# Two-layer hybrid encoder on one core: recurrent periods of layer 0 in another order on every engine, latent keys normed by columns, the last output norm inside the attention, band and maximum fused in layer 1

## What is computed

```python
# mixer A
c_kv = rmsnorm(c_kv, kv_gain)                    # 1024 rows of 128
score = einsum(w, relu(einsum(q_idx, k_idx)));   _, idx = top_k(score, 256)
p = softmax(einsum(q @ w_uk, c_kv[idx]));        o = (p @ c_kv[idx]) @ w_uv
# mixer B, per chunk of 64 rows and head (4 heads)
a_mat = strict(beta * k @ k.T * decay)
u, w = triangular_solve(a_mat + eye, [v * beta, k * beta * exp(g)])
v_new = u - w @ state
o = (q * exp(g)) @ state + (q @ k.T * decay) @ v_new
state = state * exp(g_last) + (k * exp(g_last - g)).T @ v_new
o = rmsnorm(o, out_gain) * silu(z)
# mixer D (layer 1), per chunk: keys of two chunks, 8 heads, sink per head
s = q @ k.T / 8;  s = where(valid, s, -inf);  p = softmax([s, sink])[:-1];  o = p @ v
```

## Time and profile before

| | us |
|---|---|
| median of 3 runs | 2655.8 |
| lowest, highest | 2655.26, 2657.01 |
| profiled execution: its own time | 2654.52 |
| profiled execution: span | 2652.8 |
| mean granted clock of PE over the span | 0.973 |
| busy over the span: PE, DVE, ACT, POOL | 2513.3, 1586.7, 1013.8, 213.5 |
| recurrence, first operation of PE to the last query | 359.5 to 638.7 |
| attention of layer 0 | 645 to 848 |
| window attention of layer 1 | 1798 to 1864 |

### The profile page before, as it was taken

How to read it: one execution, slowest core, us unless ns; L and a number is a source line. 1 busy time by engine, 2 the same in 40 slices (tenths; PEclk the granted TensorE clock), 3 DMA queues, 4 the chain that set the end, 5 groups by cost and what they waited for, 6 DMA issues and landing times.

```text
span 2652.8 us, 33869 instructions
## 1 busy us (share of the span) xinstructions
PE 2513.3 (95%) x13062; PEld 1976.0 (74%) x13062; DVE 1586.7 (60%) x2585; ACT 1013.8 (38%) x1816; POOL 213.5 (8%) x242
## 2 busy tenths in 40 slices
PE   7999978888988999999999998997999999999998
PEld 5587757776555878888888786784778888888787
DVE  6389966754553576565643556638577566653444
ACT  4323323444443443333332333527443333332333
POOL 4025523220000000000010000000000000000000
PEclk8999988897999999999999999999999999999999
DMA  5121100000001332222255342110232232326342
GB/s 178 39 72 44 51 10 10 2 33 1 1 24 63 96 111 90 85 86 74 83 177 184 120 155 62 34 48 17 80 127 86 66 92 84 88 82 242 129 152 102
DMA packets 207184, 217.54 MB, mean 82 GB/s; under 512 B 12496, under 2 KB 174304, under 8 KB 203568
## 3 DMA queue, kind: packets, MB, share of 16 engines
q1 hardware_dynamic: 204080, 196.13, 23.7%
q0 software_dynamic: 2944, 19.24, 2.0%
HBM read 172.35 MB, written 42.47 MB: 81 GB/s over the span
## 4 chain that ended last, share of the span: by engine, by line
PE 73%; DVE 7%; issue 3%; ACT 2%; DVEq 0%; ACTq 0%
PE ps L333 20%; PE ps L335 20%; PE ps L334 20%; PE ps L2855 2%; PE ps L2832 1%; PE ps L2843 1%; DVE met L2016 1%; PE ps L2302 1%; PE ps L2272 1%; PE ps L2240 1%; DVE d_s L1560 1%; DVE d_m L1566 1%; DVE g_XX L2627 1%; PE ps L1345 1%; PE ps L2284 1%
## 5 line engine op out<-in xcount | busy, mean ns | idle before, releaser
L322 DVE TENSOR_TENSOR wlo<-wraw,whi 128x1024 fp32r<-128x1024 f32 x152 | 185.8, 1224 | 371.5 <-ACT whi L316 371.3
L316 ACT ACTIVATE whi<-wraw 128x1024 fp32r<-128x1024 f32 x166 | 174.9, 1055 | 354.2 <-PE ps L335 337.3
L333 PE MATMUL ps<-ahi,whi 128*128 128x512 f32 x704 | 275.9, 392 | 6.3 <-DVE hT L960 4.1
L334 PE MATMUL ps<-alo,whi 128*128 128x512 f32 x704 | 274.7, 390 | 0.0
L335 PE MATMUL ps<-ahi,wlo 128*128 128x512 f32 x704 | 274.5, 390 | 0.0
L333 PE MATMUL ps<-uhi,whi 128*128 128x512 f32 x608 | 245.3, 403 | 7.7 <-DVE ulo L492 3.8
L333 PE MATMUL ps<-q_T,whi 128*128 128x512 f32 x640 | 249.2, 389 | 1.6 <-ACT upr L761 1.6
L335 PE MATMUL ps<-q_T,wlo 128*128 128x512 f32 x640 | 249.0, 389 | 0.0
L334 PE MATMUL ps<-q_T,whi 128*128 128x512 f32 x640 | 249.0, 389 | 0.0
L333 PE MATMUL ps<-q_B,whi 128*128 128x512 f32 x608 | 238.9, 393 | 2.4 <-DVE q_B L492 2.4
L334 PE MATMUL ps<-ulo,whi 128*128 128x512 f32 x608 | 238.5, 392 | 0.0
(11 more groups left out here) (457 smaller groups left out, 4589.3 us busy)
## 6 DMA issues: line engine op xcount, KB each, us to landing
wraw<-in_ffn_w_down_dram SPq DMA_DIRECT2D x88, 512.0 KB, 3.7
wraw<-in_ffn_w_gate_dram SPq DMA_DIRECT2D x44, 512.0 KB, 4.7
araw<-acts SPq DMA_DIRECT2D x88, 256.0 KB, 3.9
wraw<-in_ab_w_in_dram SPq DMA_DIRECT2D x24, 512.0 KB, 3.8
park<-hT POOLq DMA_DIRECT2D x3, 4096.0 KB, 13.2
wraw<-in_ffn_w_up_dram SPq DMA_DIRECT2D x24, 512.0 KB, 5.2
acts<-sgA SPq DMA_DIRECT2D x12, 1024.0 KB, 4.6
raw<-in_ffn_w_up_dram SPq DMA_DIRECT2D x20, 512.0 KB, 3.9
```

The source lines that it names most:

```text
L316: nc.scalar.activation(as_raw(whi[:, t.slot, :]), raw, ACT.Copy).then_inc(S("w_high"), 1)
L322: eng.tensor_tensor(as_raw(wlo[:, t.slot, :]), raw, as_raw(whi[:, t.slot, :]).bitcast(F32), ALU.subtract).then_inc(S("w_split"), 1)
L333: nc.tensor.matmul(dst, wh, xh, start=start, stop=False, **kw)
L334: nc.tensor.matmul(dst, wh, xl, start=False, stop=False, **kw)
```

## The change

In the recurrence the lists of all four engines are reordered. The bits are dealt out anew (18 in period -2; 19, 20 alone; then 21 to 28 in pairs in periods 1 to 4; 29; 30), and a period's last counts may run into the next one. `turn_out` writes to other banks and moves behind `key_rows`; `gated` moves to the end of the period; POOL's large part of `corners` waits for `first_x`. The latent keys' norms are made as 128 x 8 columns and spread through a diagonal that POOL makes. The last block's `invert`, `normed_out`, `turn_out` and `gated` and `select_threshold` move into the attention. In layer 1 the band sum, the scale and the maximum are one operation per head. Cut to its core:

```diff
@@ swa_act, swa_dve @@
-  act.activation(d_p[...], d_s[...], ACT.Exp, scale=0.125, bias=d_nm...)
+  act.activation(d_p[...], d_s[...], ACT.Exp, scale=-1.0, bias=d_nm...)
-                for a in range(2):
-                    ins = dve.tensor_tensor(d_s[:, n % 2, a:4:2, k0:192], bank(2 * (n % 2) + a)..., band..., ALU.add)
+                for h in range(4):
+                    at_ = (h // 2) * 192
+                    ins = dve.tensor_tensor_reduce(
+                        d_s[:, n % 2, h, k0:192], bank(2 * (n % 2) + h % 2)[:, at_ + k0:at_ + 192], band[:, k0:192],
+                        -0.125, 3.0e38, ALU.add, ALU.min, d_m[n % 2][:, h:h + 1])
                 ins.then_inc(S("d_biased"), 1)
                 dve.wait_ge(*after("d_biased", n + 1))
-                dve.tensor_reduce(d_m..., d_s..., AX.X, ALU.max)
-                dve.scalar_tensor_tensor(out=d_m..., in0=d_m..., scalar=0.125, in1=sink..., op0=ALU.mult, op1=ALU.max)
-                dve.tensor_tensor(d_es..., sink..., d_m..., ALU.subtract)
-                dve.tensor_scalar(d_nm..., d_m..., -1.0, None, ALU.mult)
+                dve.scalar_tensor_tensor(out=d_nm..., in0=sink..., scalar=-1.0, in1=d_m..., op0=ALU.mult, op1=ALU.min)
+                dve.tensor_tensor(d_es..., sink..., d_nm..., ALU.add)
@@ selection @@
-        EARLY = 19
-        IN_PERIOD = {-1: (19,), 0: (20, 21), 1: (22, 23), 2: (24, 25), 3: (26, 27), 4: (28,), 5: (29,), 6: (30,)}
+        EARLY = 18
+        IN_PERIOD = {-2: (18,), -1: (19,), 0: (20,), 1: (21, 22), 2: (23, 24), 3: (25, 26), 4: (27, 28), 5: (29,), 6: (30,)}
@@ ab_dve @@
-                    if i == 23:
-                        select_step(dve, bits_of(i)[0])
@@ gdn_pe @@
+        def out_bank(b):
+            return bank4({NB - 2: 2, NB - 1: 7}.get(b, 1))
+
+        def turn_out(pe, b):
+            pe.wait_ge(S("g_on"), b + 1)
+            if b < NB - 2:
+                pe.wait_ge(S("g_atc"), min(b + 4, NB))
+            elif b == NB - 2:
+                pe.wait_ge(S("g_rows"), NB)
+            else:
+                pe.wait_ge(S("g_s"), 2 * NB - 1)
...
             def spread_decay(b):
                 pe.wait_ge(S("g_atc"), b)
+                if b >= 4:
+                    pe.wait_ge(S("g_y"), b - 3)
...
-                if n == -1:
-                    key_norm_sums(pe)          # was after level_x 0
-                if n == -1:
-                    key_rows_back(pe)          # was after level_x 2
-                if O_:
-                    turn_out(n - 1)            # was after level_p 3
...
                 if A_:
                     key_rows(n + 2)
+                if n == -2:
+                    key_norm_sums(pe)
+                if n == -1:
+                    key_norm_spread(pe)
+                if O_:
+                    turn_out(pe, n - 1)
...
                 if L_:
                     make_u(n + 1)
+                if n == -1:
+                    key_rows_back(pe)
@@ key norms @@
         def key_norm_sums(pe):
             pe.wait_ge(S("kv_sq"), 1)
-            for f in range(2):
-                last = pe.matmul(bank(6 + f), ones[:, :], kv_root[:, f * HALF:(f + 1) * HALF], start=True, stop=True)
+            for b in range(NB):
+                last = pe.matmul(bank(6)[:, b:b + 1], kv_wide[:, b, :], ones[:, 0:1], start=True, stop=True)
+            last.then_inc(S("kv_sum"), 1)
+
+        def key_norm_spread(pe):
+            pe.wait_ge(S("kv_diag"), 1)
+            for f in range(2):
+                last = pe.matmul(bank(6 + f), ones[:, :], kv_wide[:, 4 * f:4 * f + 4, :]..., start=True, stop=True)
@@ gdn_act @@
-            act.wait_ge(S("kv_landed"), 16)
-            act.wait_ge(S("pb_moved"), 16)
-            act.activation(kv_root[:, :], ckvT[:, :], ACT.Square).then_inc(S("kv_sq"), 1)
...
-                    act.activation(kv_root[:, :], pair(3), ACT.Sqrt, ...)
+                    act.activation(kv_col[:, 0, :], bank(6)[:, 0:NB], ACT.Sqrt, ...)
...
+                if n == -2:                    # after decays
+                    act.wait_ge(S("kv_landed"), 16)
+                    act.wait_ge(S("pb_moved"), 16)
+                    act.activation(kv_wide..., ckvT[:, :], ACT.Square).then_inc(S("kv_sq"), 1)
...
                 if n == -1:                    # after level 2
-                    high_two(act, ("ab_out", 0))
-                    act.wait_ge(S("kv_turned"), 1)
-                    act.activation(ckvR..., pair(3), ACT.Copy)     # now at the end of the period
-                if O_:
-                    normed_out(n - 1)
+                    w_high(act, Tile(first[("ab_out", 0)]))
                 if L_:
                     level(n + 1, 3)
+                if n == -1:
+                    w_high(act, Tile(first[("ab_out", 0)] + 1))
+                if O_:
+                    normed_out(act, n - 1)
...
-            normed_out(NB - 1)
@@ gdn_pool @@
                 some(0, 1).then_inc(S("g_bt"), 1)
+                pool.wait_ge(S("g_x0"), b + 1)
                 some(1, LEVELS).then_inc(S("g_bt"), 1)
...
+                if n == -1:                    # after prepare
+                    pool.wait_ge(S("kv_rinv"), 1)
+                    pool.tensor_tensor(kv_wide[:, :, :], ident..., kv_col[:, 1, :]..., ALU.mult).then_inc(S("kv_diag"), 1)
@@ gdn_dve: the period's list after the change @@
+  add_out(n-1); masks(n+2); level 0; [n=-1: key_norm_inverse, 128x8]; select_keep of the bit left over; select_try(k)
+  differences, value_rows(n+2); [n=7: query_move 1]; counts(k,0,2) [n=0: w_low instead]; level 1
+  counts(k,2,4) [n=0: w_low, counts(k,0,1)]; level 2; add_state(n,0); weigh_gram(n+2); [n=7: query_move 3]; invert(n-1)
+  counts(k,4,5) [n=0: (k,1,3)]; level 3; counts(k,5,6), select_keep(k) [n=0: counts(k,3,4)]; select_try(k2), counts(k2,0,1)
+  level 4; first_x(n+2); [n=-1: key_norm]; counts(k2,1,2); [n=7: query_move 5]; add_state(n,1); gated(n-1)
+  [n=0: counts(k,4,6)]; counts(k2,2,6)
+  after the loop: add_out(7), query_move 7
@@ att_pe, att_act, att_dve @@
-            pe.wait_ge(S("g_y"), NB)           # was between scores(0) and scores(1); now before outs(0)
+                if n == 1:
+                    turn_out(pe, NB - 1)
+                if i == 0:
+                    normed_out(act, NB - 1)    # after exp(0)
+                if i == 0:
+                    invert(dve, NB - 1)
+                if i == 2:
+                    gated(dve, NB - 1)
+                if i == 4:
+                    select_threshold(dve)
```

More of the change, by code:

```diff
@@ L2394, in gdn_pe @@
             query(pe, 7)
-            turn_out(NB - 1)
         def query_bank(h):
@@ L2425, in key_rows_back, with normed_out @@
             last.then_inc(S("kv_turned"), 1)
+        def normed_out(act, b):
+            act.wait_ge(S("g_orinv"), b + 1)
+            for h in range(4):
+                last = act.activation(g_orow[:, h, :], g_orow[:, h, :], ACT.Identity, scale=g_orinv[:, h:h + 1])
+            last.then_inc(S("g_on"), 1)
         def gdn_act(act):
@@ L2548, in gdn_act @@
                     rows(n + 2, 2)
+                if n == -1:
+                    act.wait_ge(S("kv_turned"), 1)
+                    act.activation(ckvR[:, :, :].rearrange("p a n -> p (a n)"), pair(3), ACT.Copy).then_inc(S("kv_rows"), 1)
             query_move(act, 6, copy)
@@ L2754, in gdn_dve @@
                 if O_:
-                    gated(n - 1)
-                if mine:
+                    invert(dve, n - 1)
+                if n == 0:
+                    counts(k, 1, 3)
+                else:
                     counts(k, 4, 5)
@@ L2759, in gdn_dve @@
                     level(n + 1, 3)
-                if mine:
+                if n == 0:
+                    counts(k, 3, 4)
+                elif n >= -1:
                     counts(k, 5, 6)
-                    select_keep(dve, k)
+                    if k is not None:
+                        select_keep(dve, k)
+                        kept += 1
                 if k2 is not None:
                     select_try(dve, k2)
+                    counts(k2, 0, 1)
+                if L_:
+                    level(n + 1, 4)
                 if A_:
                     first_x(n + 2)
-                if L_:
-                    level(n + 1, 4)
-                if k2 is not None:
-                    counts(k2, 0, 4)
+                if n == -2:
+                    counts(k, 5, 6)
+                if n == -1:
+                    key_norm()
+                counts(k2, 1, 2)
                 if n == NB - 1:
@@ L2774, in gdn_dve @@
                     add_state(n, 1)
-                if k2 is not None:
-                    counts(k2, 4, 6)
-                    select_keep(dve, k2)
+                if O_:
+                    gated(dve, n - 1)
+                if n == 0:
+                    counts(k, 4, 6)
+                counts(k2, 2, 6)
+            add_out(NB - 1)
             query_move(dve, 7, dve.tensor_copy)
-            add_out(NB - 1)
-            select_threshold(dve)
```

(2 more changed lines are left out.)

114 lines of the change are left out of this document (54 added, 60 removed).

## The result

The changed kernel takes 2593.6 us (median of 4 runs, 2587.6 to 2597.0) against 2655.5 us (2654.8 to 2657.0): a ratio of 0.9764, 95% interval 0.9745 to 0.9782, so 62 us faster, where 55 were forecast (2601 us). The execution profiled is the fastest of the four, 2587.6 us (span 2585.8); the mean granted clocks of the four, fastest first, are 0.983, 0.982, 0.979 and 0.978.

The account below looks back on a forecast made before the run. TensorE was taken as the bound (73% of the chain), with gains only where it waits or runs slow. 27.5 + 4 + 4.5 + 8.5 + 1 + 3 + 6.5 = 55.0; 2655.8 - 55 = 2601 us, range 2585 to 2624.

Parts of the forecast that it names:

- Periods 1 to 5: Recurrence: TensorE waits at level_p and make_w go and full clock returns, 5.5 us a period, 27.5 us in all.
- Rival 1: Recurrence: half-height matmuls, not the wait, drop the clock, so it falls as before; gain 42, 2614 us; 17%.
- Rival 2: Recurrence: carried counts make each level wait for DVE, 2 to 4 us a period back; 2620 us; 15%.
- Rivals 4 and 5: Slower through DVE's queue, 2665 us, 2%; or reordered periods win nothing, only edges and layer 1 do, 2633 us, 3%.
- Rival 3: Periods -1, 0 and 6 run wholly at 2.4 GHz once long waits go: 13 us more, 2588 us; 13%.
- period 0: Recurrence, n = 0: make_w's wait and part of the slow clock go; 4 us, 2 to 6.
- Periods 6 and 7: Recurrence's end: about half of TensorE's idle time goes, slow clock stays; 1 us, bounds -1 and 7.
- Period -1: Before block 0: narrower reciprocal and make_w's wait gain 6.0 + 4.3, less 2.0 for key_norm and transposes; 8.5 us.
- Period -2: Recurrence's start: bit 18 is spread, so gram, turn_a and first_x come earlier; 4.5 us, 3 to 5.5.
- Last output norm: Query 7 into attention: the last block's norm leaves TensorE's 5.34 us wait; 3 us, bounds 0 and 5.
- the signs: Listed signs that the forecast is right; here, query 7 to the first turned attention tile takes 6 us.
- Layer 1: Layer 1's attention: fused operations unload DVE, ACT then bounds a step at 3.24 us; 6.5 us, 1 to 7.

Follow-up runs that it names:

- first_x alone: Kernel before the change, with first_x moved behind level 4 on DVE and POOL's large corners operation waiting for it: 2619.1 us, ratio 0.9856.
- the filled wait: Kernel before the change, with three dense 128x384 matmuls put into TensorE's wait ahead of make_w: 2640.4 us, ratio 0.9937.
- the last kernel: Changed kernel plus dense matmuls in several stretches, three small moves at the attention's start, and the latents' sums behind level_p 0: 2585.8 us, ratio 0.9724.
- the profile of 25.4 us: Changed kernel with layer 1's old sum, reduce and three small operations put back: 2604.7 us, ratio 0.9800; its period 6 took 25.36 us.
- the filled kernel: For latents' sums, apparently changed kernel plus 15 dense matmuls in periods -2 and -1: 2591.8 us; for 1.0 us waits, the filled wait: 2640.4 us.
- the three moves: Changed kernel with threshold operations ahead of the last gated product, first scores not awaiting query 7's move, exponential table loaded behind the last root: 2588.2 us, ratio 0.9732.
- invert alone: Kernel before the change, with only the output norm's reciprocal moved behind level 2, add_state and weigh_gram on DVE: 2654.6 us, ratio 0.9993.

## Why the prediction was right, and where not

- *Periods 1 to 5* (27.5 forecast, 31.5 measured): right in kind, and each wait named went. The waits gave 3.4 us a period for 3.8, short by the 0.4 that was kept in reserve. The clock was mis-sized: 2.1 was taken, by putting 1.6 us of each slow stretch into the wait and only 4.3 at half rate; the busy time shows 2.6 (first_x alone), 2.8 (the filled wait, periods 1 and 2) and 2.9 (all), the last above the upper bound of 2.8. The trace of the kernel before has none of the slow time in the wait. Its windows in period 3 are the wait, the stretch behind it, and the stretch behind that:

```profile
522.64:525.55 2.91, 0.00 (x0) 0.00 (x1) 2.81 (x6) 1.14 (x4) 0.99 (x1) 1.00 0.00 0
525.55:526.58 1.03, 1.03 (x17) 1.03 (x18) 1.03 (x3) 0.00 (x0) 0.00 (x0) 1.00 0.00 0
526.58:533.41 6.83, 6.83 (x61) 6.28 (x60) 5.70 (x15) 1.91 (x6) 1.04 (x1) 0.50 0.01 4
```

  The clock falls 0.6 to 1.9 us after the wait's end in each of the five periods, so all the slow time is paid in work: 147.67 x (1 - 0.90) = 14.8 us by the rounded mean clock, against the 14.4 by which the busy time fell. Period 23.2 us for 24.
- *Which edit did it.* The prediction gave the 2.91 us wait to first_x and the 1.00 to invert. The first is shown, and with the clock behind it makes most of the gain. invert by itself is worth nothing and costs 2.3 us at turn_out; I had seen that turn_out moves, but not that invert may depend on it.
- *Rival 1* (the clock falls as before): out, by periods 1 and 2 with the filled wait and by the five periods at 1.00 with first_x alone. *Rival 2* (DVE becomes the bound): out, TensorE waits 2.1 us in all for g_XX in six periods. *Rivals 4 and 5*: nothing of them shows.
- *Rival 3* (full clock everywhere): its 2588 us is what the profiled execution took, but not for its reason. Of the three periods that it names, period 0 did run at 1.00, and periods -1 and 6 stayed slow (0.56 and 0.78). It came from the rule of the Trainium skill that I set against the trace (TensorE: Matmul & The Clock Gate, Part 1: The HAM clock gate), that the gate follows how busy TensorE was. By the profile's busy time these runs do not bear it out: busy 9.50 of 10.30 us at 0.50 in the changed kernel's period 6, and 34.13 of 34.13 us at 0.50 in the last kernel's period -1, but 1.00 in periods 1 to 5 with 112.16 of 116.14.
- *Periods 6 and 7* (1 forecast, bounds -1 and 7; 6.6 measured, 3.5 in the profile of 25.4 us): the step that failed most. I kept the whole slow clock of the period before; the wait that went took a part of it along, and how much is left differs from execution to execution.
- *Period -1* (8.5 and 8.5) agrees by luck. The wide reciprocal put back into the changed kernel costs 3.9 us, not 6.0. first_x alone takes the stage from 36.8 to 32.8 us, 4.0 for the 4.3 that was given to make_w's wait. These two make 7.9 of the 8.5. The 2.0 us set against them, for key_norm and the eight transposes, fall into period 0 by the table's landmarks: behind make_u key_norm takes 1.28 us of DVE, and TensorE waits 0.4 us for it and transposes for 1.09. So period 0's 4.8 for 4 is a better gain than it looks, and period -1's terms without the 2.0 said 10.3. *Period -2* (4.5 and 4.2): the latents' sums were priced at 1.0 and took 3.09 at this clock (1.84 in the filled kernel, at full clock). They stand ahead of level_p 0, where the stage took 9.6 us in the last kernel, without them, for 10.7.
- *Last output norm* (3 and 1.6): the 5.3 us up to the first turned tile came as the working had them (9.38 to 4.13; the signs said 6), but 3.6 us were given back behind it, where I had priced 2.3. The threshold's operations and the exponential's table lie in the chain of the first units: the three moves took 2.1 us of waits out. The norm's move is worth 1.3 us of waits and add_out's, which I did not price, 0.8; the clock, which I did not price either, moves this stage by up to 1.5 us with the same code.
- *Layer 1* (6.5 and 9.3): right that ACT becomes the bound, wrong in its pace. I took 35.6 / 11 = 3.24 us from a profile in which ACT stands still for 0.4 us of each step; without that wait the same instructions keep it busy for 3.01. In the trace of after each instruction starts before the one ahead has ended (d_pt 0.09 us after the sink's exponential of 0.21 starts); where ACT waited, that overlap was lost, which adds to the busy time. So its busy time there was an upper bound of what it needs, not the pace itself. The fused operation of 192 columns took 0.35 us and the next started 0.28 us after its start, the figure that was taken.
- *Median against profile:* the forecast set profile against profile. The profiled execution of the changed kernel turned out 6 us under its median, that of the kernel before 1 us. Its terms are to be held against the 67 us of the profiles, not the 62 of the medians: they were 12 us short, and the total looks better than that by luck.

## What to carry to other kernels

A wait of TensorE costs more than its length when the clock falls behind it: here 2.8 us of wait cost 5.1, so look first for the waits behind which matmuls of one shape change their duration. Before moving a producer later, follow its consumer on every engine: invert moved alone gave nothing (ratio 0.9993), since the wait came back at turn_out. And when a kernel's executions scatter with the granted clock, compare stages between landmarks of the profiles, and put the clock beside each; a median of four hid a stage that was 4 us longer.

## What the runs showed that I had not expected

- The same wait does not always have the same effect on the clock. Behind 1.0 us it stayed up in the five periods of the kernel with first_x alone, but in three of five periods of the filled kernel it fell 2.0 to 2.3 us behind such a wait, for 3.4 us. Behind 1.8 us it fell in all four periods of the one profile that has them, and the other three executions of that kernel were granted more. Behind 2.3 us (invert alone, period 4) it once stayed up.
- With narrow half-height matmuls and hardly a wait TensorE stays at 1.2 GHz in some stretches (period -1, clock 0.56 at 93% busy) and not in others (periods 0 to 5, clock 1.00 at 97%). Dense fillers in period -1 went with 3 us less in one kernel and 10 more in another, which also had the sums there. In both the clock was up when the period began and fell 1.2 to 1.4 us into it; in one it was back after 3.4 us, in the other after 34.1. Why is open.
- One-column matmuls are dear: sixteen instructions took 3.41 us at 1.2 GHz (the last kernel) and 1.84 at 2.4.
